# Cross attention's head products a unit later, norms' small products at other steps, the fourth group's row numbers a block later, three loads in another order

## The reference

```python
def first_block(x, ...):                 # x: 512 x 1024
    proj = rms_norm(x) @ w_in            # RWKV-7 columns, then differential attention's q, k, v
    mix = [rwkv7_mix(proj), rms_norm(diff_attention(q, k, v))]
    h = x + rms_norm(mix @ w_out)                                  # norm 1
    u = causal_dwconv(rms_norm(h) @ w_up)                          # norm 2
    return h + rms_norm((gelu(gate) * val) @ w_down)               # norm 3

def second_block(x, mem, ...):           # mem: 256 x 1024
    x = x + gated_branch_mixer(rmsnorm(x), ...)                    # norm 4
    q = (h @ w_xq); k, v = split(rmsnorm(mem) @ w_xkv)             # 4 heads of 256
    scores = einsum('bshd,bmhd->bhsm', q, k) * (256 ** -0.5)
    o = einsum('bhsm,bmhd->bshd', softmax(scores), v)
    x = x + o @ w_xo
    x = x + hierarchical_moe(rmsnorm(x), ...)   # 16 experts in 4 groups, each token goes to two of one group
    return rmsnorm(x)
```

## Time and profile before

| | |
|---|---|
| median of 3 runs | 1635.66 us (1634.42 to 1641.47) |
| the profiled execution, its own time | 1639.76 us |
| its span (first to last instruction) | 1637.9 us |
| TensorE busy | 1518.9 us, 93% of the span |
| VectorE busy | 1098.5 us, 67% |
| ScalarE busy | 704.1 us, 43% |
| mean granted TensorE clock | 0.978 of 2.4 GHz |
| chain that ended last | PE 70%, DVE 17%, DMA 5%, ACT 4%, issue 3% |
| HBM read | 178.60 MB |

### The profile page before, as it was taken

One profiled execution on the slowest core, in us unless ns is written; L12 is line 12 of the kernel. 1 busy time (PEld: TensorE's weight loads), 2 busy tenths in 40 slices (PEclk: granted clock), 3 DMA queues, 4 the chain that ended last, 5 costly groups with the idle time before them and its releaser, 6 DMA issues.

```text
span 1637.9 us, 25699 instructions
## 1 busy us (share of the span) xinstructions
PE 1518.9 (93%) x10492; PEld 1269.0 (77%) x10492; DVE 1098.5 (67%) x1639; ACT 704.1 (43%) x1052; POOL 62.1 (4%) x53
## 2 busy tenths in 40 slices
PE   6999898988999999999999999999999888889992
PEld 4889676767887888888887887878789657888892
DVE  6831766776579827746778999456767435677875
ACT  5422434343454323323455322224335345467783
POOL 0000000000000000000000000000000000222221
PEclk9999989999999999999999999999999999989996
DMA  6230000002433223222432222224233202579894
GB/s 252 103 103 1 2 2 3 3 2 79 181 114 103 82 99 103 103 88 93 143 114 90 103 103 81 99 77 142 77 129 130 76 26 77 176 240 310 315 319 184
DMA packets 38803, 185.49 MB, mean 113 GB/s; under 512 B 6422, under 2 KB 6550, under 8 KB 24992
## 3 DMA queue, kind: packets, MB, share of 16 engines
q1 hardware_dynamic: 31648, 171.28, 30.1%
q0 software_dynamic: 4864, 8.40, 1.5%
q10 hardware_dynamic: 2176, 4.19, 0.7%
HBM read 178.60 MB, written 13.63 MB: 117 GB/s over the span
## 4 chain that ended last, share of the span: by engine, by line
PE 70%; DVE 17%; DMA 5%; ACT 4%; issue 3%; POOL 0%; SPq 0%; DVEq 0%; POOLq 0%; ACTq 0%
PE acc L507 19%; PE acc L509 19%; PE acc L508 19%; DMA raw<-wstream 4%; DVE wl L2050 2%; DVE wl L2062 1%; PE acc L1092 1%; ACT wh L1314 1%; PE acc L811 1%; PE mb L673 1%; PE mb L507 1%; ACT wh L1327 1%; PE mb L509 1%; PE mb L602 1%; PE mb L508 1%
## 5 line engine op out<-in xcount | busy, mean ns | idle before, releaser
L507 PE MATMUL acc<-XH,wh 128*128 128x512 f32 x1008 | 396.9, 394 | 3.2 <-ACT ev L1348 3.0
L509 PE MATMUL acc<-XH,wl 128*128 128x512 f32 x1008 | 392.8, 390 | 0.0
L508 PE MATMUL acc<-XL,wh 128*128 128x512 f32 x1008 | 392.6, 389 | 0.0
L1327 ACT ACTIVATE wh<-raw 128x2048 fp32r<-128x2048 f32 x99 | 189.3, 1915 | 248.1 <-DMA raw<-wstream 248.0
L2062 DVE TENSOR_TENSOR wl<-raw,wh 128x2048 fp32r<-128x2048 f32 x99 | 225.5, 2286 | 48.4 <-ACT wh L1327 45.5
L507 PEld LDWEIGHTS acc<-XH,wh 128*128 128x128 f32 x1008 | 189.3, 188 | 45.6 <-issue 6.4
L508 PEld LDWEIGHTS acc<-XL,wh 128*128 128x128 f32 x1008 | 189.4, 188 | 40.7 <-issue 2.2
L509 PEld LDWEIGHTS acc<-XH,wl 128*128 128x128 f32 x1008 | 189.3, 188 | 39.6
L1348 ACT ACTIVATE ev<-acc 128x512 f32<-128x512 f32 x146 | 85.4, 597 | 199.1 <-PE acc L509 186.1
L2050 DVE TENSOR_TENSOR wl<-raw,wh 128x1024 fp32r<-128x1024 f32 x96 | 116.3, 1221 | 32.4 <-ACT wh L1314 32.3
L1314 ACT ACTIVATE wh<-raw 128x1024 fp32r<-128x1024 f32 x96 | 101.1, 1061 | 21.4 <-DMA raw<-wstream 21.1
(11 more groups left out here) (535 smaller groups left out, 2756.5 us busy)
## 6 DMA issues: line engine op xcount, KB each, us to landing
raw<-wstream SPq DMA_DIRECT2D x99, 1024.0 KB, 4.9
raw<-wstream SPq DMA_DIRECT2D x96, 512.0 KB, 5.9
YG<-YT ACTq DMA_DIRECT2D x8, 512.0 KB, 5.8
XT<-xT SPq DMA_DIRECT2D x2, 1024.0 KB, 9.4
XT<-xT SPq DMA_DIRECT2D x1, 2048.0 KB, 8.1
GMT<-memT SPq DMA_DIRECT2D x2, 1024.0 KB, 8.6
XD<-HN SPq DMA_DIRECT2D x4, 512.0 KB, 3.2
out<-XTK SPq DMA_DIRECT2D x4, 512.0 KB, 2.6
```

The source lines that it names most:

```text
L507: mm(out_, a[0], b[0], start=start, stop=False)
L508: mm(out_, a[0], b[1], start=False, stop=False)
L509: return mm(out_, a[1], b[0], start=False, stop=stop)
L1327: actv(wh[:, n % RING].rearrange("p a b c -> p (a b c)"), raw[:, n % RING, :], ACT.Copy).then_inc(hi_done, 1)
```

## The change

The arithmetic stays the same.

1. SyncE: block 16's load stands ahead of `XT`'s, and block 17's ahead of `GMT`'s. Blocks 18 and 19 are written out ahead of the loop.
2. `norm_and_values`: norm 1's small products stand before steps 6 and 10 (were 8 and 14), norm 3's before 19 and 22 (were 15 and 20).
3. ScalarE's loops of norms 1 and 3: the second pair of values and the second rounded block stand after the eight slices, the rounding first.
4. Cross attention: each head's products, and the taking out of their results, stand a unit later, on all three engines. Odd heads' turned weights go to `ev` in place of `PTx`.
5. VectorE makes the router's weight two lowered blocks earlier, and ScalarE runs a small exponential ahead of the query's tiles.
6. `slot_rows(3)` stands before b = 3 instead of b = 2.

```diff
             sp.wait_ge(s["rk_done"], 4)
+            load(16, 0)
             sp.dma_start(XT[:, :, :], xT).then_inc(in_xb, 16)
+            load(17, 1)
             sp.dma_start(GMT[:, :, :], memT).then_inc(in_mem, 16)
...
-            load_range(16, 24)
+            load(18, 2)
+            load(19, 3)
+            load_range(20, 24)
             store_values(0)
...
-            norm_and_values(1, "v0", 8, 14)
+            norm_and_values(1, "v0", 6, 10)
...
-            norm_and_values(3, "v1", 15, 20)
+            norm_and_values(3, "v1", 19, 22)
...
+        def turned_probs(h):
+
+            return ev[:, 0:2, 2:S + 2] if h % 2 else PTx[:, :, :]
...
                 x_turn(u)
-                if u % TT == TT - 1:
-                    x_out(u // TT)
+                if u and u % TT == 0:
+                    x_out(u // TT - 1)
+            x_out(3)
...
-                    if first and b == 2:
+                    if first and b == 3:
                         slot_rows(3)
...
-                if m in (1, 5):
-                    values_out(0, m // 4)
-                    ahead(B0["v0"] + m // 4)
+                if m == 1:
+                    values_out(0, 0)
+                    ahead(B0["v0"])
+            ahead(B0["v0"] + 1)
+            values_out(0, 1)
             ahead(B0["ffn"])
...
             ahead(B0["kx"] + 3)
+            actv(sml[:, 60:61], cs("eps", 0, 1), ACT.Exp)
...
-                if i == 0 and h:
-                    act.wait_ge(s["xs_o"], 2 * h)
+                if i == 0 and h >= 2:
+                    act.wait_ge(s["xs_o"], 2 * (h - 1))
...
-                if u % TT == TT - 1:
-                    h = u // TT
-                    for v in range(2):
-                        act.wait_ge(s["xs_o"], 2 * h + v + 1)
-                        actv(XH[:, 2 * h + v, :], acc[:, v, :], ACT.Copy).then_inc(s["xs_hi"], 1)
+                if u and u % TT == 0:
+                    head_uppers(u // TT - 1)
+            head_uppers(3)
...
             lows(B0["kx"] + 3 + 3)
-            lows(B0["q"] + 3 + 3)
-
+            lows(B0["q"] + 4)
...
             dve.wait_ge(dchain, state["base"] + state["n"])
+            lows(B0["q"] + 3 + 3)
...
+                if u and u % TT == 0:
+                    head_lowers(u // TT - 1)
+            head_lowers(3)
```

More of the change, by code:

```diff
@@ L1091, in x_out @@
                     for j in range(2):
-                        last = mm(acc[:, v, :], VX[:, j, h * 256 + v * P:h * 256 + (v + 1) * P], PTx[:, j, :],
+                        last = mm(acc[:, v, :], VX[:, j, h * 256 + v * P:h * 256 + (v + 1) * P], turned_probs(h)[:, j, :],
                                   start=(j == 0), stop=(j == 1))
@@ L1684, in _ @@
                 square(32 + m, XT[:, m, :])
-                if m in (1, 5):
-                    values_out(1, m // 4)
-                    ahead(B0["v1"] + m // 4)
+                if m == 1:
+                    values_out(1, 0)
+                    ahead(B0["v1"])
+            ahead(B0["v1"] + 1)
+            values_out(1, 1)
             ahead(B0["mix"])
@@ L1800, in x_turned, with head_uppers @@
                 act.wait_ge(s["xs_t"], u + 1)
-                if i == 0 and h:
-                    act.wait_ge(s["xs_o"], 2 * h)
-                actv(PTx[:, :, i * P:(i + 1) * P], mb[:, 2 + u % 2, 0:2 * P].rearrange("p (a b) -> p a b", a=2),
+                if i == 0 and h >= 2:
+                    act.wait_ge(s["xs_o"], 2 * (h - 1))
+                actv(turned_probs(h)[:, :, i * P:(i + 1) * P], mb[:, 2 + u % 2, 0:2 * P].rearrange("p (a b) -> p a b", a=2),
                      ACT.Copy).then_inc(s["xs_te"], 1)
+            def head_uppers(h):
+                for v in range(2):
+                    act.wait_ge(s["xs_o"], 2 * h + v + 1)
+                    actv(XH[:, 2 * h + v, :], acc[:, v, :], ACT.Copy).then_inc(s["xs_hi"], 1)
             x_exp(0)
@@ L2724, in _, with head_lowers @@
             dve.wait_ge(dchain, state["base"] + state["n"])
+            lows(B0["q"] + 3 + 3)
+            def head_lowers(h):
+                for j in range(2):
+                    dve.wait_ge(s["xs_hi"], 2 * h + j + 1)
+                    v.tensor_tensor(XL[:, 2 * h + j, :], acc[:, j, :], XH[:, 2 * h + j, :].bitcast(F32),
+                                    ALU.subtract).then_inc(s["xs_done"], 1)
             x_max(0)
```

## The result

| | before | after |
|---|---|---|
| median, timed beside each other | 1639.75 us (20 runs, 1634.42 to 1644.62) | 1630.45 us (20 runs, 1625.59 to 1639.13) |
| the profiled execution, its own time | 1639.76 us | 1625.59 us |
| its span | 1637.9 us | 1623.8 us |
| ratio of the times | | 0.9946, 95% interval 0.9935 to 0.9958 |

The change saves 0.54%, 8.8 us, with 6.9 to 10.7 us by the interval. The forecast was 1623 us, and the measured 1630.45 us lies outside its range of 1617 to 1630. A second comparison gave 0.9945 (0.9931 to 0.9959). The two profiled executions differ by 14.2 us, the very sum of the forecast, and that is deceptive: 3.3 us of it lie ahead of the first edited place, where one trace has 17.1 us of half clock and the other 3.4.

A forecast was written before the change was run, and what follows sets the result against it. TensorE, busy 93% of the span, was taken as the bound. Terms 1.43 + 0 + 2.5 + 3.1 + 7.2 = 14.2 us gave 1625.5 from profiled 1639.76 or 1621.4 from median 1635.66; forecast 1623 us, range 1617 to 1630.

The forecast's parts named there:

- Loads, 1.43: Output projection: block 16, issued earlier and ahead of other transfers, ends TensorE's wait for late-rounded tiles; 1.43 us less.
- the limit of 421.6: Output projection: ScalarE must start rounding block 16 before 421.6 us for the full 1.43 us to be won.
- its own 418.5: Output projection: even landing behind `XT`, 3 MB at the row's rate would land by some 418.5 us, before the limit.
- Norm 1, 0: Norm 1: what is won at its seventh step is waited for later, that wait growing from 2.98 to some 3.5; 0 us.
- end at 483.5 as before: Norm 1: the three lowered blocks end at 483.5 us unchanged, since ScalarE rounds the last at the same time.
- Norm 3, 2.5: Norm 3: shorter wait for squares and full clock in the spread, 1.9 us, plus 0.55 at slice 6; 2.5 us less.
- slice 6: Norm 3: TensorE's wait there for a lower part behind the values and a rounding goes; 0.55 us less.
- Cross attention, 3.1: Cross attention: an earlier start, 1.33 us, and head products following a turn at once, 1.75 us; 3.1 us less.
- Experts, 7.2: First expert group: 16.06 us from b = 1 to the next group becomes 8.85, partly clock; 7.2 us less.
- rival (a): Experts: weight loads are the bound, later groups wait for blocks, only 2 of 7.2 us left; 9.0 in all; chance 0.13.
- (b): Experts and norm 3: the clock falls all the same, giving 2.9 and 1.0 us; 8.4 in all; chance 0.14.
- Rival (c): Norm 3 and cross attention: waits move and eat the gains; 6.1 us in all, 1629.6 us; chance 0.12.

## Why the prediction was wrong, by its own steps

**Loads, 1.43.** Right, in the sum (1.1 to 1.6) and in the margin: I had block 16 land at 415 on before's clock, and ScalarE began it at 410.18 + 3.3 = 413.5, 8 us ahead of the limit of 421.6. The Trainium skill (DMA: Bandwidth & Descriptors, Queues, rings and completion order) says that completion is not in the order of issue; here it was: block 16 landed by 410.2, `XT`, issued 0.38 us behind it, 9.4 us after its issue, at 415.1, and block 17 by 417.6. The prediction contradicts itself on that case: behind `XT` the block would, by its own 418.5, still have been in time, and the term 1.43 and not 0. What was not in the sum at all is the half clock that follows 90 us later, in every profile with the moved loads and nothing in the wait.

**Norm 1, 0.** Wrong: the wait behind it fell to 2.73 us instead of growing to 3.5, and the stage wins 0.53 us. The step that failed is "end at 483.5 as before": the three lowered blocks ended 21.3 us behind the first slice, and with norm 1's moves alone they end 20.8 us behind it, at 480.9 where the first slice is at 460.13. VectorE's last two of them there:

```profile
476.29 4.63 DVE L2064 TENSOR_TENSOR wl<-raw,wh 128x2048 fp32r<-128x2048 f32 x2 [0.49 <-ACT wh L1327]
```

TensorE's steps with the values also ended at 462.1, not at 463.6, which changed nothing in the sum. With the half clock that stands there in the kernel after, the stage loses 1.0.

**Norm 3, 2.5.** The steps came as forecast (sums 0.24 us late, residual 3.16 us behind, slices 8.09 us behind the sums against 8.1 forecast). But 1.2 of the 1.9 us was a half clock that stands there in 4 of 7 executions, and slice 6 gave 0.24 instead of 0.55.

**Cross attention, 3.1.** With the clock alike on both sides 3.5: start 1.4 for 1.33, heads 2.1 for 1.75. But half clock stood in the stage in 3 of 8 profiles with the old order and in all 6 with the change's parts 4 and 5, which takes 1.0 us back on average. The forecast had it alike on both sides.

**Experts, 7.2.** This is the step that failed most: "lands some 6 us after it is asked for ... lowered by 1468.9. That is also when TensorE is done". The wait for G went as forecast (0.50 for 0.6). The half block took 8.0 to 8.3 us, TensorE waited 1.43 to 3.19 us for the numbers in place of 0.65, and where the wait was short a half-clock stretch made up for it. So 4.4 to 4.6. The 6 us is near the page's median over all half blocks of the kernel before, 5.9. This half block took 8.3 us in the trace that I had, so the cost could have been read ahead: from 1460.88 it lands at 1469.2, and in the run with the row numbers alone the next group starts 3.06 us behind the start of its rounding. That gives 1472.3 instead of the forecast's 1469.4, an estimate of 2.9 us for the 2.8 that the stage fell short. The half block is asked for no earlier than before, 7.0 us behind b = 0's first product in both kernels. What moved is the time at which TensorE needs the numbers. Taking the numbers out from behind the half block ended the wait, so this cause is shown.

It is of rival (a)'s kind, as a delay of one half block. As a bound over the later groups (a) isn't shown: in the profiles without half clock there, those take 129.0 to 134.3 us with either place of the row products, 131.3 on average with the old and 132.7 with the new, and 1.4 us is within that spread.

**The sum.** 1.3 (loads) - 1.0 (norm 1) + 1.0 + 1.2 x 4/7 (norm 3) + 3.5 - 1.0 (cross attention) + 4.4 (experts) = 8.9 us; measured 8.8. That they meet to 0.1 us is luck: the measured gain is uncertain by 1.9 us, and the later groups, which the sum leaves out, vary by 5. The forecast's 14.2 is 5.3 more: 2.8 in the experts, 0.8 in norm 3, 1.0 in norm 1, 0.6 in cross attention, and 0.1 in the loads. In norm 1, norm 3 and cross attention the difference is half clock but for 0.3 us at norm 3's slice 6. I took it from one profiled execution as it stood, or did not count it at all; only the half clock in the first group was the kernel's own, 10.2 us in 6 of 8 profiles and 6.8 in the other two. Rivals (a) and (b) had the size of the whole, 9.0 and 8.4 us. Rival (c) had the time, 1629.6 us, but only because it counted from a lower start.

**Start of the count.** I put the forecast between two starts, the median of 3 runs (1635.66) and the profiled execution (1639.76). Five comparisons gave the kernel before medians of 1635.5 to 1639.75 us, the highest beside the kernel after. The forecast counts from 1623 + 14.2 = 1637.2. So of the 7.5 us between 1623 and 1630.45, 2.5 are the start, and the rest the sum.

## What to carry to other kernels

Before a stretch of half clock is counted as won, profile the kernel twice: what moves between profiles is chance and worth its average, and a stretch that repeats could here be removed by filling the idle time ahead of it as well as by moving work. When a step is moved so that another one is due earlier, don't take a usual landing time for the block that it will then wait for; ask the trace how long that very block took. And a small result that another engine waits for belongs in its engine's order ahead of work that waits for a load.

## What the runs showed that I had not expected

With two loads in the output projection moved, a half-clock stretch stands 90 us later in 11 of 11 profiles with nothing in the wait ahead of it, against 1 of 7 without the move; the cause stays open. The largest stretch hangs on idle time: with 24 unused products in a wait of 3.4 us, 10.2 us of half clock went and the stage took 18.74 us for 22.74, in the one profile of that kernel. Chance in the clock is large in this kernel: the unedited attention has between 3.4 and 17.1 us of half clock from one execution to the next (227.6 to 232.8 us).
